# Attention of a hybrid decoder layer: two units per visit of the matmul engine, scores in four banks, dense work on one

## The reference

```python
u = rms_norm(h, norm1_gain)
hq, hf, hi, hg, aq, ak, av = split(u @ w_in)
o_rec = hgrn2_mixer(hq, hf, hi, hg, lb, out_gain)       # 4 recurrent heads, 128x128 state each
o_att = swa_sink_mixer(aq, ak, av, q_gain, k_gain, sinks)
h = h + concat(o_rec, o_att) @ w_out
u = rms_norm(h, norm2_gain)
h = h + (silu(u @ w_gate) * (u @ w_up)) @ w_down        # D_FF = 2816

# swa_sink_mixer: 8 query heads in 2 groups of 4, 2 key/value heads of 64, blocks of 128 queries
scores = einsum('bnqhgd,bnkhd->bnhgqk', qb, kb)          # each block sees itself and the one before
scores = where((rel >= 0) & (rel < 128) & (kpos >= 0), scores, -1e30)
m = maximum(max(scores), sink)
p = exp(scores - m);  denom = sum(p) + exp(sink - m)
out = einsum('bnhgqk,bnkhd->bnqhgd', p / denom, vb)
```

## Time and profile before

| | |
|---|---|
| median of 3 runs | 1091.58 us (1091.49 to 1091.92) |
| profiled execution | 1091.61 us, its span 1089.6 us |
| PE | busy 1078.6 us (99%), 6322 matmuls |
| PEld | 882.9 us (81%) |
| DVE | 667.0 us (61%) |
| ACT | 508.6 us (47%) |
| POOL | 376.1 us (35%) |
| granted TensorE clock, mean | 0.998 |
| attention | 135.9 to about 201 us of the span |

### The profile page before, as it was taken

The page is one execution under the profiler, slowest core; times in us unless marked ns, Lnnn a source line. Parts: engine busy times, 40 slices in busy tenths (PEclk is TensorE's granted clock), DMA queues, the critical chain, the costliest instruction groups (busy, mean ns, idle before and its releaser), DMA issues.

```text
span 1089.6 us, 16140 instructions
## 1 busy us (share of the span) xinstructions
PE 1078.6 (99%) x6322; PEld 882.9 (81%) x6322; DVE 667.0 (61%) x814; ACT 508.6 (47%) x807; POOL 376.1 (35%) x337
## 2 busy tenths in 40 slices
PE   9999999999999999989999999999999999999998
PEld 9998867778878787877888888888888877888886
DVE  7314588579698957995243433334343688787776
ACT  8414457656576635453333333333333554545531
POOL 0301133200000007226536444553645742534462
PEclk9999999999999999999999999999999999999999
DMA  7101100011115133113313313331332785455433
GB/s 290 40 1 58 40 20 21 21 43 37 40 35 180 31 115 147 39 43 125 129 51 126 126 62 122 114 129 47 126 126 67 268 313 160 139 156 164 128 104 155
DMA packets 37387, 112.73 MB, mean 103 GB/s; under 512 B 4929, under 2 KB 9793, under 8 KB 35905
## 3 DMA queue, kind: packets, MB, share of 16 engines
q1 hardware_dynamic: 36880, 111.38, 29.8%
q10 hardware_dynamic: 432, 0.33, 0.1%
HBM read 83.12 MB, written 28.57 MB: 103 GB/s over the span
## 4 chain that ended last, share of the span: by engine, by line
PE 90%; DVE 5%; issue 2%; ACT 1%; DMA 1%; POOL 0%; SPq 0%; DVEq 0%; ACTq 0%; POOLq 0%
PE ps L1353 28%; PE ps L1355 27%; PE ps L1354 27%; PE ps L1541 1%; PE ps L1568 1%; DVE olo L1760 1%; PE ps L1583 1%; PE ps L1585 1%; DVE h L1755 1%; PE ps L1588 1%; PE ps L1525 1%; DMA wraw<-wo_a 1%; PE ps L1594 1%; PE ps L1511 1%; PE ps L1392 0%
## 5 line engine op out<-in xcount | busy, mean ns | idle before, releaser
L1727 DVE TENSOR_TENSOR glo<-graw,ghi 128x1024 fp32r<-128x1024 f32 x21 | 26.2, 1246 | 147.9 <-POOL s34raw L696 147.6
L1353 PE MATMUL ps<-uhi,whi 128*128 128x512 f32 x272 | 112.2, 413 | 0.0
L1355 PE MATMUL ps<-uhi,wlo 128*128 128x512 f32 x272 | 106.3, 391 | 0.0
L1354 PE MATMUL ps<-ulo,whi 128*128 128x512 f32 x272 | 106.2, 391 | 0.0
L2103 DVE TENSOR_TENSOR yacc<-ps,yacc 128x512 f32<-128x512 f32 x104 | 68.4, 681 | 10.0 <-PE ps L1355 9.9
L1353 PE MATMUL ps<-ubhi,arhi 128*128 128x512 f32 x176 | 69.1, 393 | 0.8 <-DVE arlo L2078 0.5
L1353 PE MATMUL ps<-ohi,s12hi 128*128 128x512 f32 x168 | 66.3, 395 | 3.1 <-DVE olo L1760 2.5
L1354 PE MATMUL ps<-ublo,arhi 128*128 128x512 f32 x176 | 68.6, 390 | 0.0
L1355 PE MATMUL ps<-ubhi,arlo 128*128 128x512 f32 x176 | 68.5, 389 | 0.0
L1353 PE MATMUL ps<-ohi,s34hi 128*128 128x512 f32 x168 | 65.5, 390 | 0.8 <-ACT ps L1187 0.8
L1354 PE MATMUL ps<-olo,s12hi 128*128 128x512 f32 x168 | 65.9, 392 | 0.0
(11 more groups left out here) (335 smaller groups left out, 2944.1 us busy)
## 6 DMA issues: line engine op xcount, KB each, us to landing
hidden<-hst SPq DMA_DIRECT2D x11, 1792.0 KB, 6.0
ubraw<-hidden SPq DMA_DIRECT2D x33, 512.0 KB, 5.4
graw<-wg SPq DMA_DIRECT2D x21, 512.0 KB, 4.4
uraw<-wu SPq DMA_DIRECT2D x21, 512.0 KB, 3.5
wraw<-wproj SPq DMA_DIRECT2D x17, 512.0 KB, 3.5
araw<-wd SPq DMA_DIRECT2D x22, 384.0 KB, 4.7
h<-xT SPq DMA_DIRECT2D x8, 512.0 KB, 4.9
h_kept<-h SPq DMA_DIRECT2D x16, 256.0 KB, 2.2
```

Source lines behind the costliest of these rows:

```text
L1353: nc.tensor.matmul(out, whi_, xhi_, start=first, stop=False, skip_group_check=seeded)
L1354: nc.tensor.matmul(out, whi_, xlo_, start=False, stop=False, skip_group_check=seeded)
L1355: return nc.tensor.matmul(out, wlo_, xhi_, start=False, stop=last, skip_group_check=seeded)
L1727: nc.vector.tensor_tensor((glo2 if g == 2 else glo[g % 2])[:, :], graw[g % 2][:, :], ghi[g % 2][:, :].bitcast(F32), ALU.subtract).then_inc ...
```

## The change

Attention is walked in visits of two units. A visit holds SN(i − 2), TR(i − 4), AE(i − 5), TR(i − 3), SN(i − 1), PV(i − 6), PV(i − 5), SC(i), SC(i + 1), SE(i), SE(i + 1) for i = 0, 2, ..., 20, and the number of dense parts before each of the first ten is written out in `VISIT_PARTS`. The eleventh visit (i = 20) stands among the first steps of head 0, in the place of the last unit step before.

For this, score units alternate between banks 3, 4 and banks 1, 2, and a unit waits for the mask of the unit two before it. The dense groups 11 to 14 leave banks 1 and 2 and use bank 0, as group 15 does anyway, so that groups 12 to 15 wait for the group just before to be read out; groups 16 and 17 wait for all masks. `sc` has four buffers in place of three, `pT` two in place of one, and TR(i)'s readers wait for PV(i − 2) in place of PV(i − 1). `pT` now lies on the place of the later `A` of head 0, so POOL clears `A` after the last PV and not after the last TR. The diff, cut to its core (the other lines replace 3 by `N_SC` in the numbers of buffers):

```diff
+VISIT_PARTS = (1, 2, 2, 2, 2, 2, 1, 1, 2, 2)
+N_SC = 4
...
-    steps = []
-    for i in range(units + LAG + 1):
-        steps.append([s for s in (("SN", i - 2), ("AE", i - LAG - 1), ("TR", i - LAG), ("PV", i - LAG - 1), ("SC", i),
-                                  ("SE", i - 1)) if 0 <= s[1] < units])
-    order += mix(take(13), steps[:units], lead=1) + mix(take(4), steps[units:units + LAG])
+    visits = []
+    for i in range(0, units + 2 * LAG, 2):
+        visits.append([s for s in (("SN", i - 2), ("TR", i - 4), ("AE", i - 5), ("TR", i - 3), ("SN", i - 1),
+                                   ("PV", i - 6), ("PV", i - 5), ("SC", i), ("SC", i + 1), ("SE", i), ("SE", i + 1))
+                       if 0 <= s[1] < units])
+    for parts, visit in zip(VISIT_PARTS, visits):
+        order += mix(take(parts), [visit], lead=parts)
...
-    steps = [steps[units + LAG], [("HK", 0)], [("HQ", 0)], [("HS", 0), ("H2", 0)], [("HM", 0)], [("HD", 0)],
+    steps = [visits[-1], [("HK", 0)], [("HQ", 0)], [("HS", 0), ("H2", 0)], [("HM", 0)], [("HD", 0)],
...
-        sc = at("sc", 167, [P, 3, GRP, P + 1])
-        vstep = at("vstep", 183, [P, NC, P])
+        sc = at("sc", 167, [P, N_SC, GRP, P + 1])
+        vstep = at("vstep", 182.75, [P, NC, P])
...
-        pT = at("pT", 179, [P, 2, GRP * P])
+        pT = [at(f"pT{i}", kb, [P, 2, GRP * P]) for i, kb in enumerate((179.125, 175.125))]
...
+        def proj_bank(g):
+            return 0 if 11 <= g < 15 else g % 3
+        def score_bank(i):
+            return (3, 1)[i % 2]
...
-                        pool.wait_ge(s_tr, 2 * NC)
+                        pool.wait_ge(s_pv, 2 * NC)
                         nc.gpsimd.memset(A[:, :], 0.0).then_inc(s_setup, 1)
...
                         act.wait_ge(s_pte1, i + 1)
-                        act.wait_ge(s_pv, i)
+                        act.wait_ge(s_pv, i - 1)
...
-                        pe.wait_ge(*((s_vev, NC + g + 1) if g < 3 else (s_pev, g - 2)))
+                        if g < 3:
+                            pe.wait_ge(s_vev, NC + g + 1)
+                        elif 12 <= g < 16:
+                            pe.wait_ge(s_pev, g)
+                        else:
+                            pe.wait_ge(s_pev, g - 1 if g == 11 else g - 2)
+                        if 16 <= g < 18:
+                            pe.wait_ge(s_masked, 2 * NC)
...
+                    elif i == 1:
+                        pe.wait_ge(s_pev, 11)
                     else:
-                        pe.wait_ge(s_masked, i)
+                        pe.wait_ge(s_masked, i - 1)
...
-                        outs = [ps[:, 3 + g, j * 2 * P:(j + 1) * 2 * P] for g in range(KVH)]
+                        outs = [ps[:, score_bank(i) + g, j * 2 * P:(j + 1) * 2 * P] for g in range(KVH)]
...
-                    if i:
-                        dve.wait_ge(s_pv, i)
+                    if i >= 2:
+                        dve.wait_ge(s_pv, i - 1)
```

More of the change, by code:

```diff
@@ L257, in build @@
         rtok = small[:, 88:96]
-        smax = at("smax", 207, [P, 36])
-        nmax, den, rden = (smax[:, 12 * i:12 * i + 12] for i in range(3))
+        smax = at("smax", 207, [P, 12 * N_SC])
+        nmax, den, rden = (smax[:, 4 * N_SC * i:4 * N_SC * (i + 1)] for i in range(3))
         uhi = at("uhi", 7, [P, KT, T], F32R)
@@ L705, in sink_column @@
             def sink_column(i):
-                return nc.gpsimd.tensor_copy(sc[:, i % 3, :, P].rearrange("p (g j) -> p g j", g=KVH),
+                return nc.gpsimd.tensor_copy(sc[:, i % N_SC, :, P].rearrange("p (g j) -> p g j", g=KVH),
                                              sink.rearrange("p (g u j) -> p g u j", g=KVH, u=2)[:, :, i % 2, :])
@@ L755, in _ @@
                     i = step[1]
-                    r = i % 3
+                    r = i % N_SC
                     pool.wait_ge(s_rden, i + 1)
@@ L760, in _ @@
                                             .broadcast_to([P, GRP, P]), ALU.mult).then_inc(s_prob, 1)
-                    if i + 3 < 2 * NC:
-                        sink_column(i + 3).then_inc(s_sinkc, 1)
+                    if i + N_SC < 2 * NC:
+                        sink_column(i + N_SC).then_inc(s_sinkc, 1)
                 elif step == ("SC", 0):
@@ L765, in _ @@
                     pool.wait_ge(s_const, 16 * N_CONST)
-                    for i in range(3):
+                    for i in range(N_SC):
                         sink_column(i)
@@ L1015, in _ @@
                         act.wait_ge(s_pte1, i + 1)
-                        act.wait_ge(s_pv, i)
-                        nc.scalar.activation(pT[:, 0, :], ps[:, 5 + i % 2, :], ACT.Copy).then_inc(s_pte0, 1)
+                        act.wait_ge(s_pv, i - 1)
+                        nc.scalar.activation(pT[i % 2][:, 0, :], ps[:, 5 + i % 2, :], ACT.Copy).then_inc(s_pte0, 1)
                 elif kind == "AE":
@@ L1438, in _ @@
                         t = slice(half * HALF, (half + 1) * HALF)
-                        mm = three(ps[:, g % 3, :], whi[u % 2][:, w], wlo[u % 2][:, w], uhi[:, k, t],
+                        mm = three(ps[:, proj_bank(g), :], whi[u % 2][:, w], wlo[u % 2][:, w], uhi[:, k, t],
                                    ulo[:, k, t], k == 0, k == KT - 1)
@@ L1524, in _ @@
                     for j in range(GRP):
-                        mm = nc.tensor.transpose(ps[:, 5 + i % 2, j * P:(j + 1) * P], sc[:, i % 3, j, 0:P], ident[:, :])
+                        mm = nc.tensor.transpose(ps[:, 5 + i % 2, j * P:(j + 1) * P], sc[:, i % N_SC, j, 0:P], ident[:, :])
                     mm.then_inc(s_tr, 1)
@@ L1541, in _ @@
                             mm = nc.tensor.matmul(ps[HD * g:HD * g + HD, 7, pair * 2 * P:(pair + 1) * 2 * P], vals,
-                                                  pT[:, t, g * 2 * P:(g + 1) * 2 * P],
+                                                  pT[i % 2][:, t, g * 2 * P:(g + 1) * 2 * P],
                                                   start=(t == 1), stop=(t == 0 or n == 0))
@@ L1828, in _ @@
                             dve.wait_ge(s_on, hh - 1)
-                    nc.vector.tensor_tensor(dst, ps[:, g % 3, :], rs[:, cols], ALU.mult).then_inc(s_pev, 1)
+                    nc.vector.tensor_tensor(dst, ps[:, proj_bank(g), :], rs[:, cols], ALU.mult).then_inc(s_pev, 1)
                 elif kind == "E":
@@ L1861, in _ @@
                     i = step[1]
-                    r = i % 3
+                    r = i % N_SC
                     dve.wait_ge(s_scm, i + 1)
                     sv = sc[:, r, :, 0:P]
-                    pv = ps[:, 3:5, :].rearrange("p b (j n) -> p (b j) n", j=2)
+                    pv = ps[:, score_bank(i):score_bank(i) + 2, :].rearrange("p b (j n) -> p (b j) n", j=2)
                     if i == 0:
@@ L1868, in _ @@
                     if i >= 2:
-                        if i >= 3:
-                            dve.wait_ge(s_tr, i - 2)
+                        if i >= N_SC:
+                            dve.wait_ge(s_tr, i - N_SC + 1)
                         nc.vector.tensor_copy(sv, pv[:, :, 0:P]).then_inc(s_prev, 1)
@@ L1877, in _ @@
                     nm = nmax[:, 4 * r:4 * r + 4]
-                    if i >= 3:
-                        dve.wait_ge(s_sinkc, i - 2)
+                    if i >= N_SC:
+                        dve.wait_ge(s_sinkc, i - N_SC + 1)
                     nc.vector.tensor_reduce(nm, sc[:, r, :, :], AX.X, ALU.max, negate=True).then_inc(s_amx, 1)
@@ L1882, in _ @@
                     i = step[1]
-                    q4 = slice(4 * (i % 3), 4 * (i % 3) + 4)
+                    q4 = slice(4 * (i % N_SC), 4 * (i % N_SC) + 4)
                     dve.wait_ge(s_exp, 4 * (i + 1))
@@ L1889, in _ @@
                     dve.wait_ge(s_tr, i + 1)
-                    if i:
-                        dve.wait_ge(s_pv, i)
-                    nc.vector.tensor_tensor(pT[:, 1, :].rearrange("p (j q) -> p j q", q=P),
+                    if i >= 2:
+                        dve.wait_ge(s_pv, i - 1)
+                    nc.vector.tensor_tensor(pT[i % 2][:, 1, :].rearrange("p (j q) -> p j q", q=P),
                                             ps[:, 5 + i % 2, :].rearrange("p (j q) -> p j q", q=P),
```

## The result

The changed kernel takes 1085.81 us (median of 4 runs, 1084.99 to 1086.98) beside 1091.68 for the kernel before on the same chip: a ratio of 0.9944, interval 0.9932 to 0.9957. Applied to 1091.58 that is 1085.5 us, with 1084.2 to 1086.9 as its interval.

The account below looks back on a forecast made before the run. PE's own path was taken as the bound. Fewer shape changes (3.73) and removed waits (1.53) made 5.26 us, less 0.3 for new waits: 5.0 off 1091.61, so 1086.6 us, range 1085.6 to 1089.4.

Parts of the forecast that it names:

- What bounds it, and the direction: Whole run: PE holds 90% of the chain of waits, so time off PE's path shortens the run, by 5.0 us.
- the price of PV behind another PV: PE in attention: a second value product straight behind the first takes 0.96 us, against 1.01 behind transposes.
- the allowance for waits: PE in attention after the change: 0.3 us of new waits, allowed because DVE's spare is thin.
- the missing 1.53 us: Attention before the change: 65.28 us less 63.75 of summed prices, taken as PE waits in the first units, all removed.
- A change of shape, not of tile: PE in attention: only changing array shape costs, about 0.20 into scores or dense; fewer changes save 3.73 us.
- rival (c): PE in attention: entry prices belong to each step, so only 2.0 us is gained, 1089.6; chance 0.08.
- The DVE walk: Attention: DVE's operations timed from the end of PV 5 keep up with PE, at least 0.5 us spare.
- (a): Attention: waits, from DVE's lag in one-part visits or the fill, take 1.4 us, leaving 3.6, 1088.0; chance 0.15.
- rival (e): Attention: DVE becomes the bound, at 3.6 us a unit giving 1093.2, deciding from about 3.5; chance 0.05.
- a visit covers each boundary: Dense groups on one bank: a visit of 1.59 to 4.44 us covers each eviction of 0.2 + 0.69.
- (d): Dense groups on one bank: four boundaries wait about 0.9 us each, 3.6 in all, giving 1090.2; chance 0.03.
- Head 0: After attention: DVE's chain arrives 0.45 us later relative to PE, fits with 0.6 left, so nothing is lost.

Follow-up runs that it names:

- e2: Changed kernel with its new banks and buffers kept but the old order of one unit a visit; 1092.56 us, ratio 1.0004 to the kernel before.
- e5: Changed kernel with TR and PV alternating inside a visit (TR, PV, TR, PV); 1088.5 us, ratio 0.9968 to the kernel before.
- e6: Changed kernel with DVE doing the masked copy of every second unit twice; 1090.25 us, ratio 0.9988 to the kernel before.
- e4: Changed kernel with one dense part more ahead of the first visit, so three dense group ends fall inside dense blocks; 1099.06 us, ratio 1.0066.
- e3: Changed kernel with pairs on the old two score banks and dense groups in three banks; 1106.91 us, ratio 1.0137 to the kernel before.

## Why the prediction was off, step by step

**What bounds it, and the direction: right.** PE's own path was the thing to count. e2 shows that nothing else in the change moves the time, and the 65.28 became 59.56, where 60.02 and 0.3 of waits were forecast.

**The step that failed is the price of PV behind another PV, with the allowance for waits beside it.** I put 0.96 on it, from 168.32 − 167.84 = 0.48 for four, as if that were an inner step. It wasn't: those four open the shape. In the trace after, the steps of a pair are 0.48, 0.43, 0.43 and 0.54 (157.76 to 159.64): the opening costs 0.05 and is paid once, a step that neither opens nor closes takes 0.43, and a pair takes 1.88, not 1.97. So a PV behind another costs 0.87 instead of 0.96. Seven pairs make 0.63. In the kernel before every first four stand behind TR or dense work and every second four end the block, so no row there shows a step that neither opens nor closes, and 0.48 should have stood as an upper bound only. e5 confirms it from the other side, where each PV again opens, at 0.49.

The 0.3 us for waits were not needed; PE waits for nothing in attention. Nor were the missing 1.53 us of the kernel before all waits: the two waits lengthen their steps by 0.69 (145.44 − 143.85 = 1.59 for an SC of 0.90) and 0.37 (152.89 − 151.03 = 1.86 for a dense part of 1.49), 1.06 in all. The other 0.47 was work that the prices had too low, half of it PV. The forecast did not suffer, since 65.28 was read and not added up, but its split did: of the 5.72 won 4.66 are shapes and 1.06 are waits, not 3.73 and 1.53.

The other terms stand close: a dense part behind another 1.36, not 1.38 (0.14 more gain over seven), a pair of score units 1.62, not 1.59 (0.24 less over eight). A dense opener with the TR behind it takes 2.02, as I had it, though the timeline, which goes by starts, splits it 1.49 and 0.53 where the chain splits it 1.58 and 0.44. So 60.02 − 0.63 − 0.14 + 0.24 = 59.49 against 59.56, and with the 0.3 the stretch gained 5.72 instead of 5.0. The range's bottom had 0.9 below the forecast, 0.3 for no waits and 0.6 for openings that cost less (27 × 0.02 is 0.54). By the stretch alone the time would be 1091.58 − 5.72 = 1085.9, inside the range; what it had no room for is the scatter of the timings on top, 1085.5 and 1086.3 for the same kernel. On which side of the bottom the first of them fell was chance; that the gain was put too low was not.

**A change of shape, not of tile, is what costs: right.** Score units follow each other at 0.12 and TR behind TR at 0.11 for each transpose. The Trainium skill (TensorEngine Tiling (Array Packing), Key Properties) says that switching the tiling mode, not just the tile, drains TensorE; the 0.12 and e5's 0.30 agree with it, and rival (c), 2.0 us of gain, is out.

**The DVE walk: right in its times, wrong in what I concluded of its spare.** With zero at the end of PV 5 (166.96), SC 12 was due at 174.92 and came at 175.00, reciprocal 11 at 174.72 and came at 174.79, the eviction of P 14 at 179.12 and came at 179.21. So (a) is out. But I said that DVE "idles some 4 us" and would be about 90% busy. Over the stretch it is busy 49.44 of 59.56 us, 83%, but from 145 to 185 it is busy 38.28 of 40, 96%: its idle time lies at the ends. 3.1 us of it (1.75, 1.21 and 0.17) come behind the last score unit, where they help nobody, and the 1.44 of the fill come before there is work to do ahead. e6 shows what is left: 1.5 us. So, as an estimate, rival (e) would begin to cost from about 2.92 + 1.5 / 16 = 3.01 a unit, and turn the sign from 2.92 + (5.7 + 1.5) / 16 = 3.37, not from 3.5. It did not come, because no DVE operation of a unit grew beside POOL (a copy still takes 0.69, a reciprocal 0.17), but it was nearer than argued.

**Banks: right that a visit covers each boundary** (no wait after, 7.1 us in e4), too cheap in what (d) would have cost. **Head 0: right**, the idle of 1.03 went to 0.39, where 0.6 was walked; the table load's lead came out 0.15 shorter than walked.

## What to carry to other kernels

Where an engine alternates between kinds of work and each change has a price, take the opening price from a row that opens and the inner price from a row that does not; where the trace of before has no row of the second kind, say so and keep the price as a bound. Batching two units is worth the saved openings only if each unit of the batch has its own output bank: on one pair of banks the same order lost 15 us instead of winning 6. And count a second engine's spare only up to its last operation that somebody waits for.

## What was not expected of the hardware

The granted clock fell in the middle of the kernel behind waits of 3.1 and 3.2 us on PE (e4), and in a stretch with eight waits of up to 2 us (e3), to windows of 0.66, with eight transposes at 1.91 instead of 1.03 us. The waits of e3 added up to 12.5 us and the loss to 19.3, of which 3.9 are steps at the lower clock; those of e4 added up to 7.1 and the loss to 11.4, with 2.6 in such steps. In the changed kernel's own attention, with no wait, the clock stays at 1.00. So in these two runs the loss was about half as much again as the waits themselves, and not all of that was clock.
